# Six activation tiles placed 32 bytes further on, and the first down chunk's output tiles taken in another order

## The reference, cut to what matters

```python
x = x + jnp.einsum('bse,ed->bsd', mixed, w_out[l])            # out
x = x + memory_cross_attention(...)                           # co: its last product, with w_co
h = rms_norm(x, norm_g)
x = x + (jax.nn.silu(h @ w_gate) * (h @ w_up)) @ w_down       # x0 (gate and up), down0
...
x = x + _gla_mixer(...)                                       # go: its last product, with gla_w_out
u = _causal_depthwise_conv(h @ w_up, conv_w) + conv_b         # f1 and f2: h @ w_up of the two layers
gate, up = jnp.split(u, 2, axis=-1)
return (jax.nn.gelu(gate, approximate=False) * up) @ w_down
```

## Time and profile before

| | |
|---|---|
| median of 3 runs | 1045.52 us (1045.42 to 1045.61) |
| profiled execution, device time | 1047.69 us |
| its span in the profile | 1045.9 us |
| PE busy | 1037.0 us, 7330 matmuls |
| DVE busy | 862.9 us |
| ACT busy | 671.2 us |
| chain that ended last | PE 80%, DVE 13%, ACT 4% |
| granted TensorE clock | 1.0 (the 2.4 GHz level) in all stretches |

### The profile page before, as it was taken

How to read it: one execution, slowest core, us unless ns; L and a number is a source line. 1 busy time by engine, 2 the same in 40 slices (tenths; PEclk the granted TensorE clock), 3 DMA queues, 4 the chain that set the end, 5 groups by cost and what they waited for, 6 DMA issues and landing times.

```text
span 1045.9 us, 19060 instructions
## 1 busy us (share of the span) xinstructions
PE 1037.0 (99%) x7330; PEld 959.6 (92%) x7330; DVE 862.9 (83%) x1083; ACT 671.2 (64%) x952; POOL 2.7 (0%) x8
## 2 busy tenths in 40 slices
PE   8999999999999999999999999999999999999998
PEld 8888999898888999999899999999899889999998
DVE  6878986687787856998998888798998899888886
ACT  6666565466555446676786767675546678667673
POOL 0000000000000000000000000000000000000000
PEclk9999999999999999999999999999999999999999
DMA  9942463354555564534655655464333565555541
GB/s 344 283 152 81 163 219 142 121 196 167 180 194 201 178 224 160 191 130 156 217 186 201 211 190 176 165 215 162 126 121 117 171 232 176 191 205 201 191 148 64
DMA packets 30529, 186.91 MB, mean 179 GB/s; under 512 B 3735, under 2 KB 6520, under 8 KB 8840
## 3 DMA queue, kind: packets, MB, share of 16 engines
q1 hardware_dynamic: 29896, 185.05, 50.6%
q10 hardware_dynamic: 576, 1.05, 0.3%
HBM read 183.96 MB, written 1.34 MB: 177 GB/s over the span
## 4 chain that ended last, share of the span: by engine, by line
PE 80%; DVE 13%; ACT 4%; issue 2%; DMA 1%; SPq 0%; DVEq 0%; ACTq 0%
PE g L551 52%; PE d L551 28%; DVE w_lo L1573 4%; ACT w_hi L1083 1%; DVE x L1570 1%; ACT hy_scores L1083 1%; DVE p_both L1577 1%; DMA raw<-weights 1%; DVE sq_sum L1570 1%; PE d L554 0%; DVE scores L1577 0%; DVE scores L1567 0%; DVE row_max L1660 0%; DVE hy_conv L1577 0%; DVE gla_both L1577 0%
## 5 line engine op out<-in xcount | busy, mean ns | idle before, releaser
L1573 DVE TENSOR_TENSOR w_lo<-raw,w_hi 128x2048 fp32r<-128x2048 f32 (+1 forms) x175 | 389.3, 2227 | 59.3 <-ACT w_hi L1083 59.0
L1083 ACT ACTIVATE w_hi<-raw 128x2048 fp32r<-128x2048 f32 (+1 forms) x174 | 324.6, 1871 | 58.6 <-PE d L551 41.4
L551 PE MATMUL g<-f_both,w_hi 128*128 128x512 f32 x704 | 246.1, 393 | 0.0
L551 PE MATMUL g<-f_both,w_lo 128*128 128x256 f32 x704 | 197.0, 280 | 0.0
L551 PEld LDWEIGHTS g<-f_both,w_hi 128*128 128x128 f32 x704 | 131.8, 187 | 29.0
L551 PE MATMUL d<-hid_hi,w_hi 128*128 (+1 forms) x528 | 146.9, 278 | 0.0
L551 PE MATMUL d<-hid_lo,w_hi 128*128 (+1 forms) x528 | 146.8, 278 | 0.0
L551 PE MATMUL d<-hid_hi,w_lo 128*128 (+1 forms) x528 | 146.8, 278 | 0.0
L551 PEld LDWEIGHTS g<-f_both,w_lo 128*128 128x128 f32 x704 | 132.9, 189 | 0.1
L551 PEld LDWEIGHTS d<-hid_hi,w_hi 128*128 128x128 f32 x528 | 99.9, 189 | 0.9
L551 PEld LDWEIGHTS d<-hid_lo,w_hi 128*128 128x128 f32 x528 | 99.2, 188 | 0.0
(11 more groups left out here) (388 smaller groups left out, 2231.8 us busy)
## 6 DMA issues: line engine op xcount, KB each, us to landing
raw<-weights SPq DMA_DIRECT2D x168, 1024.0 KB, 4.8
bias_tab<-bias_dram SPq DMA_DIRECT2D x8, 192.0 KB, 7.6
x<-x_t ACTq DMA_DIRECT2D x4, 256.0 KB, 5.4
raw<-weights SPq DMA_DIRECT2D x4, 256.0 KB, 6.6
raw<-weights SPq DMA_DIRECT2D x2, 512.0 KB, 7.6
mem_t<-mem_t SPq DMA_DIRECT2D x1, 1024.0 KB, 9.7
out<-x SPq DMA_DIRECT2D x3, 256.0 KB, 2.2
hy_swap<-hy_qk SPq DMA_DIRECT2D x4, 128.0 KB, 6.1
```

The lines of the kernel that those rows point to most:

```text
L551: return pe.matmul(out, lhsT, rhs, start=start, stop=stop, skip_group_check=True)
L1083: return act.activation(out, in_, func, **kw)
L1573: return dve.tensor_tensor(out, a, b, ALU.subtract)
```

## The change

It makes two edits. In the layout, `out_both`, `co_both`, `x0_both`, `f1_both`, `go_both` and `f2_both` begin 32 bytes further on; `gla_both` and `mem_both` stay at +0 and `in_both`, `hy_both`, `p1_both` and `p2_both` at +32. In `chunk_k`, the order of the output tiles is a parameter, and the first chunk of `down0` takes tiles 0, 1, 2, 3, 6, 7, 4, 5, that is banks D[0], D[1], D[3], D[2]. All other calls keep 0 to 7. No instruction is added or removed.

```diff
-        out_both, OUT = parts_at("out_both", A_AT)
-        co_both, CO = parts_at("co_both", A_AT)
-        x0_both, X0 = parts_at("x0_both", B_AT)
+        out_both, OUT = parts_at("out_both", A_AT + 32)
+        co_both, CO = parts_at("co_both", A_AT + 32)
+        x0_both, X0 = parts_at("x0_both", B_AT + 32)
...
-        f1_both, F1 = parts_at("f1_both", A_AT)
+        f1_both, F1 = parts_at("f1_both", A_AT + 32)
...
-        go_both, GO = parts_at("go_both", B_AT)
-        f2_both, F2 = parts_at("f2_both", A_AT)
+        go_both, GO = parts_at("go_both", B_AT + 32)
+        f2_both, F2 = parts_at("f2_both", A_AT + 32)
...
-            def chunk_k(c, slot, moving, k0, first, final, to_x):
+            def chunk_k(c, slot, moving, k0, first, final, to_x, tiles=range(KT)):
...
-                order = [(h, f) for f in range(KT) for h in range(2)] if final else [(h, f) for h in range(2) for f in range(KT)]
+                order = [(h, f) for f in tiles for h in range(2)] if final else [(h, f) for h in range(2) for f in tiles]
...
-                    chunk_k(j + FIRST["down0"], (FIRST["down0"] + jm) % U, (hid_hi, hid_lo), j * 2, first, final, True)
+                    tiles = (0, 1, 2, 3, 6, 7, 4, 5) if first else range(KT)
+                    chunk_k(j + FIRST["down0"], (FIRST["down0"] + jm) % U, (hid_hi, hid_lo), j * 2, first, final, True, tiles)
```

## The result

The changed kernel takes 1049.83 us (median of 5 runs, 1049.46 to 1050.37), the kernel before in the same comparison 1045.46 (1045.40 to 1045.61): the two medians are 4.4 us (0.42%) apart, and the ratio on record is 1.0035, with an interval from 1.0024 to 1.0045. Predicted were 1034.9 us with a range from 1032.0 to 1043.5. The sign was wrong, and the time lies outside the range.

A forecast was written before the change was run, and what follows sets the result against it. PE was taken as the bound, busy 99% of the span. Pairs -8.0, last chunks -0.45, down0's order -2.5 and hand-overs +0.3 gave -10.65 us, from the median 1045.5 to 1034.9 us, range 1032 to 1043.5.

The forecast's parts named there:

- The 60 ns of the 13th matmul: In down0, the 13th matmul started some 60 ns late, waiting for DVE; the new order would remove this.
- late at the 19th: Sign to check in down0: D[2] is now wanted at the 19th matmul, which should not start late.
- The last chunks of out, co and go: Their 144 matmuls of 256 columns would go from 120.0 to 116.9 ns each, 0.45 us less.
- slow stretches that turn fast: Slow stretches of out, go and f2 that turn fast would add up to 1 us of gain.
- the +0.3: Time given back where shorter chunks of out, co and go meet DVE at hand-overs: 0.3 us.
- pairs at distance 32: 1200 pairs (512 and 256 columns) in x0, f1, f2, out, co, go: 6.7 ns less each, 8.0 us.
- twice 13.4: A pair's extra over its columns' time at distance 0, 26.9 ns, read as the same extra on each matmul.
- Rival 5: Slow rhythm takes hold of the pairs in the loops of x0, f1 and f2: 1049.4 us; chance 0.06.
- The order in down0: Without the stall at the 13th matmul, down0's 530 matmuls take 60.16 us, 2.5 us less.
- Rival 2: The order does nothing, as another short stall in down0 sets the slow rhythm again: 1037.4 us; chance 0.06.
- The base of the sum: The profiled execution lay 2.2 us over the runs' median; the forecast subtracted its gain from the median, 1045.5 us.
- the third rival: Placement does nothing for pairs, only the order (and 0.15 to 0.45 us) is left: 1042.8 us; chance 0.07.

The follow-up runs named there:

- e1: The kernel before, unchanged, profiled and timed once more: ratio 1.0006 (0.9994 to 1.0018).
- E6: New tile order in down0 and only x0 at +32, against the kernel before: 1047.45 us, ratio 1.0017.
- e9: New tile order in down0 and only f1 and f2 at +32, against the kernel before: 1049.83 us, ratio 1.0023.
- e2: New tile order in down0 alone, all six tiles back at +0, against the kernel before: 1046.87 us, ratio 1.0005.
- e12: The kernel before, unchanged, a single execution with a profile: 1047.65 us.
- e5: The changed kernel run again, against the kernel before: 1049.72 us, ratio 1.0040.
- e3: The six tiles at +32 alone, with the old tile order in down0, against the kernel before: 1047.72 us, ratio 1.0016.
- e7: New tile order in down0 and only out, co and go at +32, against the kernel before: 1046.99 us, ratio 1.0015.
- e14: New tile order alone, all six tiles at +0, a single execution with a profile: 1046.72 us.
- e13: New tile order alone, all six tiles at +0, another single execution with a profile: 1045.36 us.

## Why the prediction was wrong

**What held.** PE was the bound and stayed it. The 60 ns of the 13th matmul went as forecast, and none was late at the 19th. The last chunks of out, co and go came to 116 to 118 ns a matmul: with their 0.15 us each, out and co give the -0.3 of the table. Go gave 0.45, since its pairs, slow before (353 ns), are at 347 now; the prediction had not counted that. Together -0.74, against the -0.45 of that step. The prediction did say that slow stretches that turn fast would add up to 1 us; besides go, the 96 pairs ahead of the loop of f2 gave 0.6 and the first 32 of x0 0.17. Of the +0.3, what shows at the hand-over to x0 is 0.04: the first matmul of x0 is 278 ns ahead of the second in the changed kernel and 234 in e1.

**The step that failed: pairs at distance 32.** The prediction took "the same 3.3 ns off either matmul of a pair", -8.0 us for 1200 pairs. Measured in the loops: 228.8 + 118.3 = 347.1 ns against 230.2 + 116.7 = 346.9. The long matmul gains 1.4 and the short one loses 1.6. Its ground was that the extra over the columns' time is a sum of one term per matmul that depends on the distance only. But at distance 0 the short matmul behind a long one had 116.7, not 120.0, in the trace of before already: 230.2 against 226.7 was the other half of that. The sum of the pair fitted "twice 13.4", and its two parts did not; the starts within one pair would have shown it.

**The step that was missing: what the pairs hand over.** Rival 5 had the slow rhythm taking hold of the big loops, at 1049.4 us, near the measured time, but it put it in the pairs. It sits in the down chunks, whose operands nobody moved, and which stand nowhere in the sum. The chain of one turn in f1 is 0.20 us longer in the chunk of `hid` and 0.01 in the pairs. Ten of 11 such chunks in each of f1 and f2 were fast, which is 2.0 us for each, and the chunk of `p_hi` and `p_lo` behind them, of the same shape, goes from 5.44 to 5.65 too. E6 and e9 show that it follows the pairs that come before.

**The order in down0.** The step said that without the stall the stretch takes 60.16 us, 2.5 less. Without it, and with x0 at +0, it takes 59.95 (e2, -2.35 to e12) in some executions and 61.64 in others. With x0 at +32 it takes 62.19 in all three profiles (the changed kernel, e5 and e6), since the edit to x0 brings PE in slow and the edit to the order removes the stall that could have ended it (e3: 60.03). The two edits, neither of which costs anything in down0 in the profile that has it alone (e2, e3), cost 2.2 us together. Rival 2 (another short stall sets the rhythm again) was right in kind and had 0.06; its stall was at the loop's entry and not at a semaphore.

**The base of the sum.** The profile of before lay 2.2 us over the median, and the prediction noted it and went on. The difference was down0's slow rhythm itself (62.30 us in the profile of before, 60.03 in e1): by their times, the runs that made the median did not have the loss that the step wanted to remove. Against them the most that it could gain was 0.1 us (60.03 to 59.95).

**The account.** The changed kernel's profile less e1's, from the phases: down0 +2.16, f1 +2.35, f2 +1.76, against -0.29 (out, co), -0.17 (x0), -0.45 (go) and -1.4 in p1, gla and p2, the phases behind f1 and f2. The sum is +3.9, and the spans differ by 3.8. Of the 1.4, 1.2 come with f1 and f2 at +32 alone (e9), and the waits of PE show where: in e2 it waits 0.6 us for DVE's `gla_both` and twice 0.3 for `sq_sum`, at the heads of gla, p1 and p2, and in e9 for neither. The reading, not tested by itself, is that the slower down chunks ahead of them leave DVE that much more time. So the three phases with the slow rhythm cost 6.3 us, and the others gave 2.3 back.

**The skill.** The prediction weighed a sentence of the Trainium skill, page "SBUF — State Buffer", section "Who interferes with whom", that "PE and ACT never wait on anyone". That sentence is about engines that wait for each other; no effect of placement, the third rival at 1042.8, was what the prediction drew from it. The runs don't agree with that consequence: one loop at four distances takes 346.9 to 353 ns a pair. That the cause is a port of SBUF is not shown either.

**Open.** What the rhythm is in the hardware, why a stall of the same length turns it in one execution and not in the next, why the pairs of x0 stay slow in e7's profile, what its lower group and the upper groups of e3 and of go at +32 consist of, and what decides the head of f2.

## What to carry to other kernels

Where an engine is full and the gain is to come from a few ns a matmul, a matmul's distance to the next is no property of the matmul alone: measure the exact sequence, with what runs before and behind it, before multiplying by its count. If a profile lies off the median of the timed runs by more than the effect in question, profile again and subtract phase by phase first, since the loss to be removed may be that difference. Where the runs of one kernel form two groups, a variant is judged beside the old kernel in the same comparison, and the groups are compared one by one. A short stall removed at one place can come back where the next thing is just in time, here at the entry of a loop; look at what the late engine's sequencer gains by waiting.

## What the runs showed of the hardware that was not expected

- The same matmuls (256 columns, `hid`) run at 113.3 or 117.8 ns, at the same granted clock, through all 528 of down0. Which one it is depends on what PE did before, and a delay of 0.09 us (e14) to 0.17 us (e12) began the slow one, one of 0.12 (e3) ended it, and delays of the same lengths left it as it was (e13, e1).
- Pairs of 512 and 256 columns at distance 0 also run at 346.9 or at 353 ns (e7: 353 through 320 pairs of x0, where e1 has 346.7).
- With weights loaded, a pair in the loop of f1 takes 346.9, 347.1, 353 and 350.3 ns at distances 0, 32, 64 and 96 of the operands' addresses modulo 128 bytes.
- The first matmul of a rolled loop took 206 ns to the next start in place of 113, where the sequencer's register operation began 0.15 us ahead of it (e2, e14), and 113 where it began 0.34 us ahead (e1).
- The down chunks take the rhythm from the pairs ahead of them: behind pairs of 230.2 + 116.7 ns they take 5.45 us, behind 231.7 + 115.0 and behind 228.8 + 118.3, whose sums are the same to 0.4 ns, 5.65.
